# The triangular inverse of the gated delta rule on four quadrants of the array, head by head

## What is computed

```python
m = jnp.where(strict, jnp.einsum('nbhid,nbhjd->nbhij', kb, kc) * decay, 0.0)
eye = jnp.eye(CHUNK, dtype=f32)
t_inv = lax.linalg.triangular_solve(eye + m, jnp.broadcast_to(eye, m.shape), left_side=True, lower=True)
u = t_inv @ (vc * bc[..., None])
w = t_inv @ (kb * jnp.exp(gcum)[..., None])
```

## Time and profile before

| | |
|---|---|
| median of 3 runs | 2931.18 us |
| profiled execution | 2928.76 us |
| its span | 2927.0 us |
| TensorE matmul busy | 96% |
| VectorE busy | 79% |
| ScalarE busy | 50% |
| mean granted TensorE clock | 0.983 |
| share of the four inverses' levels in the span | 71.0 us, 2.4% |

### The profile page before, as it was taken

The page is one execution under the profiler, slowest core; times in us unless marked ns, Lnnn a source line. Parts: engine busy times, 40 slices in busy tenths (PEclk is TensorE's granted clock), DMA queues, the critical chain, the costliest instruction groups (busy, mean ns, idle before and its releaser), DMA issues.

```text
span 2927.0 us, 61890 instructions
## 1 busy us (share of the span) xinstructions
PE 2806.4 (96%) x24636; PEld 2724.2 (93%) x24636; DVE 2298.7 (79%) x3646; ACT 1469.2 (50%) x2438; POOL 476.1 (16%) x515
## 2 busy tenths in 40 slices
PE   5999989999999998999999999999999899999998
PEld 5999888999999998889999998899988899999998
DVE  7999767679978786666898998889887789777654
ACT  3445535554454464455545446644677544544632
POOL 0016012030110210200203112201036300202201
PEclk9999999999999999999999999999999999999999
DMA  9995403458968752135687895489532489677354
GB/s 341 350 361 202 143 15 116 137 178 323 356 223 287 238 179 88 45 109 180 234 328 280 291 337 191 137 306 356 166 100 73 144 289 343 234 270 245 126 185 136
DMA packets 173160, 632.26 MB, mean 216 GB/s; under 512 B 19216, under 2 KB 19600, under 8 KB 172560
## 3 DMA queue, kind: packets, MB, share of 16 engines
q1 hardware_dynamic: 124128, 450.82, 43.6%
q10 hardware_dynamic: 48816, 178.41, 17.3%
HBM read 628.10 MB, written 1.05 MB: 215 GB/s over the span
## 4 chain that ended last, share of the span: by engine, by line
PE 83%; DVE 10%; ACT 4%; DMA 1%; issue 1%; POOL 0%; ACTq 0%; DVEq 0%; SPq 0%
PE psum L602 24%; PE psum L603 24%; PE psum L604 24%; DVE w_lo L572 3%; DVE qkv L1432 1%; ACT w_hi L560 1%; DVE xl L2708 1%; PE psum L1816 1%; PE psum L1819 1%; DMA raw<-stream_dram 1%; PE psum L2806 1%; PE psum L2826 1%; PE psum L2820 1%; PE psum L1805 1%; ACT sm L2302 1%
## 5 line engine op out<-in xcount | busy, mean ns | idle before, releaser
L602 PE MATMUL psum<-h_hi,w_hi 128*128 128x256 f32 (+1 forms) x4464 | 1268.0, 284 | 2.7 <-DVE w_lo L572 1.6
L603 PE MATMUL psum<-h_hi,w_lo 128*128 128x256 f32 (+1 forms) x4464 | 1261.3, 283 | 0.0
L604 PE MATMUL psum<-h_lo,w_hi 128*128 128x256 f32 (+1 forms) x4464 | 1259.2, 282 | 0.0
L572 DVE TENSOR_TENSOR w_lo<-raw,w_hi 128x1024 fp32r<-128x1024 f32 x852 | 1074.3, 1264 | 172.2 <-ACT w_hi L560 171.2
L560 ACT ACTIVATE w_hi<-raw 128x1024 fp32r<-128x1024 f32 x852 | 876.0, 1055 | 360.7 <-DMA raw<-stream_dram 166.4
L602 PEld LDWEIGHTS psum<-h_hi,w_hi 128*128 128x128 f32 x4464 | 850.2, 190 | 11.0 <-DVE w_lo L572 3.8
L604 PEld LDWEIGHTS psum<-h_lo,w_hi 128*128 128x128 f32 x4464 | 848.2, 190 | 0.0
L603 PEld LDWEIGHTS psum<-h_hi,w_lo 128*128 128x128 f32 x4464 | 847.1, 190 | 0.8 <-issue 0.7
L602 PE MATMUL psum<-u_hi,w_hi 128*128 128x256 f32 x1584 | 441.4, 279 | 1.3 <-ACT length L1145 1.3
L604 PE MATMUL psum<-u_lo,w_hi 128*128 128x256 f32 x1584 | 441.2, 279 | 0.0
L603 PE MATMUL psum<-u_hi,w_lo 128*128 128x256 f32 x1584 | 441.2, 279 | 0.0
(11 more groups left out here) (452 smaller groups left out, 3522.9 us busy)
## 6 DMA issues: line engine op xcount, KB each, us to landing
raw<-stream_dram SPq DMA_DIRECT2D x852, 512.0 KB, 4.2
ada_w<-ada_dram ACTq DMA_DIRECT2D x328, 512.0 KB, 5.0
tmp<-c_dram ACTq DMA_DIRECT2D x8, 512.0 KB, 4.1
x<-x_dram SPq DMA_DIRECT2D x1, 1024.0 KB, 10.0
ctx_x<-ctx_dram ACTq DMA_DIRECT2D x1, 1024.0 KB, 4.7
means<-means_dram ACTq DMA_DIRECT2D x1, 1024.0 KB, 4.7
out_dram<-tmp SPq DMA_DIRECT2D x4, 256.0 KB, 2.5
const<-const_dram SPq DMA_DIRECT2D x1, 785.0 KB, 13.4
```

The costliest lines, as they stand in the source:

```text
L572: p.nc.vector.tensor_tensor(p.w_lo[:, slot].rearrange("p k m -> p (k m)"), p.raw[:, slot], p.w_hi[:, slot].rearrange("p k m -> p (k m)").b ...
L602: mm(out, p.w_hi[:, slot, k], hi, start=start, stop=False, skip_group_check=skip)
L603: mm(out, p.w_lo[:, slot, k], hi, start=False, stop=False, skip_group_check=skip)
L604: return mm(out, p.w_hi[:, slot, k], lo, start=False, stop=stop, skip_group_check=skip)
```

## The change

The transposed inverse of a half is now kept on the *other* half's partitions: low blocks' on 64 to 127, high blocks' on 0 to 63. The plain inverse stays on its own half. So the first product goes from low rows to high columns and back, and the second products use all four quadrants: for the transposed inverse within a half, for the plain one across. The masks carry the minus sign. The plain inverse is summed in PSUM (banks 4 to 7, `start=False`), and ScalarE copies it to SBUF after each level (`levels` in `gdn_scalar`, new). The transposed one is still added by VectorE. All hand-overs inside the levels are per head instead of per pair: VectorE has four masks and four additions of 128x128 per level, unrolled, and TensorE waits per head for `t_ready` (ScalarE), `inv_grown` and `new_ready` (VectorE). The first turns go straight to banks 4 to 7, for which TensorE waits on `pairs_used` or `turned_used`. The sines move from `gdn` to `up`, behind the split of tile 6, and VectorE's wait for them moves down to just ahead of the rotary scaling.

```diff
-    put("masks", np.concatenate(masks, 1))
+    put("masks", -1.0 * np.concatenate(masks, 1))
...
     def levels(gq):                                   # gdn_vector
-        with dve.Fori(0, LEVELS) as level:
-            for b in range(PAIRS):
-                both = slice(2 * b, 2 * b + 2)
-                dve.wait_ge(p.sem["lp_done"], level * PAIRS + (at("lp_done", MERGES) + b + 1))
...
-            for b in range(PAIRS):
-                dve.wait_ge(p.sem["lq_done"], level * PAIRS + (at("lq_done", MERGES) + b + 1))
-                grown = p.tmp[:, 2 * b : 2 * b + 2].rearrange("p i n -> p (i n)")
-                v.tensor_tensor(grown, grown, p.psum[:, 4 + b], ALU.subtract).then_inc(p.sem["inv_grown"], 1)
+        for level in range(LEVELS):
+            for i in range(GROUP):
+                dve.wait_ge(p.sem["lp_done"], at("lp_done", MERGES) + level * GROUP + i + 1)
+                v.tensor_tensor(
+                    p.new_h[:, i], p.psum[:, i, 0:P].rearrange("p (c n) -> p c n", c=2),
+                    masks[:, level].unsqueeze(1).broadcast_to([P, 2, HALF]), ALU.mult,
+                ).then_inc(p.sem["new_ready"], 1)
+            for i in range(GROUP):
+                dve.wait_ge(p.sem["lq_done"], at("lq_done", MERGES) + level * GROUP + i + 1)
+                t_t = p.tmp[:, i, 0:P]
+                v.tensor_tensor(t_t, t_t, p.psum[:, i, P:T], ALU.add).then_inc(p.sem["inv_grown"], 1)
...
     def first(gq):                                    # gdn_scalar
+        for i in range(GROUP):
+            act.wait_ge(p.sem["first_turned"], a("first_turned") + gq * GROUP + i + 1)
+            f(p.tmp[:, i, P:T], p.psum[:, 4 + i, 0:P], ACT.Copy).then_inc(p.sem["t_ready"], 1)
+
+    def levels(gq):
+        for level in range(LEVELS):
+            for i in range(GROUP):
+                act.wait_ge(p.sem["lq_done"], a("lq_done") + gq * MERGES + level * GROUP + i + 1)
+                f(p.tmp[:, i, P:T], p.psum[:, 4 + i, 0:P], ACT.Copy).then_inc(p.sem["t_ready"], 1)
...
     def inverse(gq):                                  # gdn_tensor
+            if gq or i < 2:
+                pe.wait_ge(p.sem["pairs_used"], a("pairs_used") + 2 * (gq * GROUP + i + (0 if gq else 2)) + 2)
+            else:
+                pe.wait_ge(p.sem["turned_used"], a("turned_used") + i + 1)
+            for c in range(2):
+                for e in range(2):
+                    ins = mm(p.psum[halves[e], 4 + i, c * HALF : c * HALF + HALF], p.inv_h[halves[1 - e], i, 0, c],
+                             ident[halves[1 - e], halves[1 - e]], start=c == 0, stop=c == 1, skip_group_check=True)
+            ins.then_inc(p.sem["first_turned"], 1)
+        pe.wait_ge(p.sem["turned_used"], at("turned_used", 4) + 4)
+        for level in range(LEVELS):
+            for i in range(GROUP):
+                pe.wait_ge(p.sem["t_ready"], at("t_ready", COPIED) + level * GROUP + i + 1)
+                if level:
+                    pe.wait_ge(p.sem["inv_grown"], at("inv_grown", GROWN) + PAIRS + (level - 1) * GROUP + i + 1)
+                for c in range(2):
+                    for e in range(2):
+                        at_c = c * P + e * HALF
+                        ins = mm(p.psum[halves[1 - e], i, c * HALF : c * HALF + HALF],
+                                 p.a_t[halves[e], i, at_c : at_c + HALF], p.inv_h[halves[e], i, 1, c], start=True, stop=True)
+                ins.then_inc(p.sem["lp_done"], 1)
+            for i in range(GROUP):
+                pe.wait_ge(p.sem["new_ready"], at("new_ready", MERGES) + level * GROUP + i + 1)
+                for c in range(2):
+                    to = slice(c * HALF, c * HALF + HALF)
+                    for e in range(2):
+                        other = halves[1 - e]
+                        t_t, new = p.inv_h[other, i, 0, c], p.new_h[other, i, c]
+                        mm(p.psum[other, i, P + c * HALF : P + c * HALF + HALF], new, t_t, start=True, stop=True)
+                        ins = mm(p.psum[halves[e], 4 + i, to], t_t, new, start=False, stop=True, skip_group_check=True)
+                ins.then_inc(p.sem["lq_done"], 1)
...
-    if st.layer == 0:                                 # gdn_scalar
-        trig_scalar(p, act)
+    levels(1)
...
+            if j == 6 and st.layer == 0:              # up_scalar
+                trig_scalar(p, act)
...
-    dve.wait_ge(p.sem["trig_done"], 1)                # up_vector, at its head
...
     dve.wait_ge(p.sem["up_sq"], a("up_sq") + 12)
+    dve.wait_ge(p.sem["trig_done"], 1)
```

More of the change, by code:

```diff
@@ L1541, in scores @@
                     ins = v.tensor_tensor(
-                        p.new_h[part, both],
+                        p.new_h[HALF - HALF * e : P - HALF * e, both],
                         p.a_t[part, both].rearrange("p i (c n) -> p i c n", c=2)[:, :, :, HALF * e : HALF * e + HALF],
@@ L1729, in gdn_scalar @@
     first(0)
+    levels(0)
     corners(0)
@@ L1789, in inverse @@
+        merged = LEVELS * GROUP
+        for i in range(GROUP):
+            if i % 2 == 0:
+                pe.wait_ge(p.sem["t_ready"], at("t_ready", COPIED) + merged + i + 2)
+                pe.wait_ge(p.sem["inv_grown"], at("inv_grown", GROWN) + PAIRS + merged - GROUP + i + 2)
             for c in range(2):
                 to = slice(i % 2 * P + c * HALF, i % 2 * P + c * HALF + HALF)
-                for part in halves:
-                    ins = mm(p.psum[part, PAIR_BANKS[gq][i // 2], to], p.inv_h[part, i, 0, c], ident[part, part], start=True, stop=True)
@@ L1793, in inverse @@
[L1793 to L1798, removed]
-                if i % 2 == 0:
-                    pe.wait_ge(p.sem["inv_grown"], level * PAIRS + (at("inv_grown", GROWN) + i // 2 + 1))
-                for c in range(2):
-                    to = slice(i % 2 * P + c * HALF, i % 2 * P + c * HALF + HALF)
-                    for e, part in enumerate(halves):
-                        at_c = c * P + e * HALF
-                        ins = mm(p.psum[part, i // 2, to], p.a_t[part, i, at_c : at_c + HALF], p.inv_h[part, i, 1, c],
-                                 start=True, stop=True)
-                if i % 2:
-                    ins.then_inc(p.sem["lp_done"], 1)
-            for i in range(GROUP):
-                if i % 2 == 0:
-                    pe.wait_ge(p.sem["new_ready"], level * PAIRS + (at("new_ready", MERGES) + i // 2 + 1))
-                for c in range(2):
-                    to = i % 2 * T + c * HALF
-                    for part in halves:
-                        t_t, new = p.inv_h[part, i, 0, c], p.new_h[part, i, c]
-                        mm(p.psum[part, 4 + i // 2, to : to + HALF], new, t_t, start=True, stop=True)
-                    for part in halves:
-                        t_t, new = p.inv_h[part, i, 0, c], p.new_h[part, i, c]
-                        ins = mm(p.psum[part, 4 + i // 2, to + P : to + P + HALF], t_t, new, start=True, stop=True)
-                if i % 2:
-                    ins.then_inc(p.sem["lq_done"], 1)
@@ L1822, in inverse @@
[L1822 to L1828 removed]
+                ins = mm(p.psum[low, i // 2, to], p.a_t[low, i, c * P + HALF : c * P + P], p.inv_h[low, i, 1, c],
```

37 lines of the change are left out of this document (12 added, 25 removed).

## The result

The kernel after the change takes 2918.56 us (median of five runs, 2911.19 to 2919.12), beside 2932.48 us for the kernel before (median of five, 2930.19 to 2933.94 and one single execution of 6984.86, which the ratio leaves out). The ratio is 0.995 (95% interval 0.9935 to 0.9966): 14.7 us faster by the ratio, 13.9 by the medians, where the prediction said 30.4. The direction was right, the size less than half. The profiled execution is 2918.56 us with a span of 2916.8 us.

A forecast was written before the change was run, and what follows sets the result against it. TensorE was taken to bound each level, with 0.55 us of hand-over on top. Levels 6.85 us plus entry, 7.5 us, times four 30; plus 0.5 clock, less 0.1 sines: 30.4 off 2931.18 gives 2900.8 us, range 2896 to 2918.

The forecast's parts named there:

- Four wide: Second products of a level run on four quadrants at once: 0.93 us per level instead of 1.86; forecast's chance 68%.
- rival A: Shared output partitions let only two quadrants run: 2.78 to 2.8 us per level, 2918 us in all; chance 14%.
- B: TensorE takes records no faster than a floor, at 25 ns a level of 2.53 us, 2913 us in all; chance 10%.
- C: Quadrants ending in the same PSUM partitions go one after another: 4.65 us per level, 2955 us in all; chance 6%.
- Level of 1.95 us: One merging level of the inverse, 3.33 us before, takes 1.95 us: TensorE's 1.86 and some of VectorE's 2.1.
- Hand-over per head: Inside a level, VectorE's eight smaller operations let heads go on singly, removing TensorE's 0.55 us wait for a pair.
- TensorE per level: 1.86 us four wide: TensorE's products in each of five levels per inverse: first products 0.93 us, second products 0.93 us.
- Loop unrolled: Writing out VectorE's level loop: only its 0.07 us register steps go, worth nothing.
- Entry: Ahead of the levels, each head waits for its own copy only, so first products start 0.65 us earlier per inverse.
- Clock: Three of four inverses ran partly at half clock, costing 1.3, 1.2 and 2.1 us; 0.5 us counted back in all.
- Sines and copies: Moving the sines on ScalarE costs 0.1 us; ScalarE's 20 copies per inverse, 0.2 to 0.3 us each, are covered.

The follow-up runs named there:

- the turned loop: Kernel after, TensorE's levels in a hardware loop whose body begins with a level's second products and ends with the next level's first: 2898.35 us, ratio 0.9883.

## Why the prediction was right and wrong

**Four wide: right.** The rival A (two wide), B (a floor of 25 ns per record) and C (collision) are out: four records start in 0.06 us, 14.6 ns a record, with pairs of quadrants that write the same partitions of PSUM (in different banks, the transposed product in bank i and the plain one in 4 + i). The prediction weighed three rules of the Trainium skill against this: on loads and row groups ("TensorE: Matmul & The Clock Gate", Part 3), on row tiles in one PSUM bank ("TensorEngine Tiling (Array Packing)", Gotcha 1) and on a floor of about 25 ns from start to start ("TensorE: Matmul & The Clock Gate", Part 1). At 14.6 ns a record over the four quadrants, none of the three holds between quadrants in this trace.

**Level of 1.95 us: right where no stop falls.** 1.86 and 1.90 us in the trace. Eight operations of VectorE at 0.23 us from start to start are 1.87 us, TensorE's products also, and the two are level, as forecast.

**Hand-over per head: right.** The step put it at 0.55 us a level; handing over by pairs again cost 0.52 to 0.56.

**"TensorE per level: 1.86 us four wide", five times in each inverse: the step that failed.** It took for granted that 192 records and loads and their waits can reach TensorE in that time, in every level. The item "Loop unrolled" priced VectorE's register steps alone; TensorE's levels were written out before as well. The sum had no term for the code of these products, although the profile before showed both halves of it: the instruction queue's 154 packets of 2.52 MB, and a level of 192 instructions in 3.33 us. At 1.87 us a level the code is used up 256 instructions in 2.34 us, and the next 256 were ready only 3.76 to 4.23 us after the last. A level with a stop took 3.13 and 3.31 us for the 1.95 of the sum, and the four stretches 55.1 us for the 39 that it implies; without the stops they took 44.5. Of the rivals, A has the number that came (2918) with a mechanism that isn't there, which is luck; B was nearest in kind, a limit that no stretch before was dense enough to show, but its 25 ns per record are refuted.
The Trainium skill ("Runtime: NRT & Kernel Launch", "Instruction fetch mechanics") says that code is brought in blocks of 256 instructions, that crossing a block costs little and is mostly hidden, since the sequencer issues slower than blocks arrive, and that a jump to code outside the current two blocks waits for it, one reason why kernels prefer full unrolling. On the size the trace agrees. On the cost of a crossing it disagrees here: the three in the levels of the first inverse stood for 1.2 to 1.9 us. And the preference doesn't hold for this code: the turned loop is 20 us faster than the unrolled levels.

**Entry: 0.65 us was 0.23.** The step from the turns to the first products shrank as said, from 1.21 us to 0.51, 0.70 less:

```profile
375.87 0.68 PE L1799 MATMUL psum<-const,tmp 64*64 64x64 f32 x16 [0.80 <-DVE tmp L1549]
...
376.38 0.28 PE L1811 MATMUL psum<-tmp,a_t 64*64 64x64 f32 x4
```

But the turns themselves start at 375.87, not 375.40, since VectorE's first inverse comes later in this execution. Its size is within the spread of executions.

**Clock: right in kind, too small.** Two of the four windows after are at 0.88 and 0.87, two at 1.00, where before three were at 0.86 to 0.90. The forecast counted 0.5 us back; the third inverse alone gained its 1.2 us. This error goes against the miss.

**Sines and copies: right.** The sines measured 1.0006. ScalarE's copies run beside VectorE's additions and release nothing last.

## What to carry to other kernels

When a change makes an engine's work denser, count its instructions per microsecond, not only their time: here TensorE's straight code held at 256 instructions in 4.4 us and stopped at 256 in 2.3 us. Idle time put down to no semaphore, with the same count of instructions between one stop and the next, was a wait for code here, and a loop around the same instructions removed it; where the code was slow enough before, the loop gave nothing. Whether a loop pays depends on both sides: its jump cost 0.3 to 0.4 us a level here, the stops more. Hand-over in smaller pieces can be worth more than fewer, longer operations, also on an engine that is nearly full.

## What the runs showed of the hardware

- TensorE's code came in loads of 16,384 bytes, 256 instructions, and code ran 2.3 to 2.9 us after a load's start; the sequencer then had the next 256 ready only 3.76 to 4.23 us after the last.
- Four 64x64 quadrants took records 14.6 ns apart together, each quadrant one in 58 ns. Between quadrants records started out of the program's order.
- A jump back in TensorE's loop with three counting registers cost 0.3 to 0.4 us a turn (2.19 and 2.26 us a level for 1.87), after the change; in the kernel before, with two registers, 0.6 us for the four turns of an inverse (17.2 us for 16.6).
- A semaphore wait on two satisfied conditions cost TensorE 94 ns (90 us for 960).
- At a granted clock of 1.00 one product of 128x256 took 117 ns from start to start in most stretches and 113 ns in others of about 50 us, many of them at other places in each execution of one program.
